# Turning rows 0 to 4 of a layer's input by VectorE blocks and a trip over DRAM instead of by TensorE

## The chip, the cores and the metric

One core of a Trainium2 chip runs the whole program. The metric is the device time of one execution in microseconds (us), as the median of several executions. Five engines work side by side: TensorE (PE, with its weight loads shown as PEld), VectorE (DVE), ScalarE (ACT), GpSimd (POOL) and SyncE (SP), which here only issues DMAs. The engines wait for one another by semaphores.

## The reference

A two-layer decoder trunk on 1024 prompt tokens and 32 sample tokens (8 sequences of 4), model width 1024, in float32. Layer 0 is a gated short convolution, layer 1 a gated linear recurrence with 8 heads of 128.

```python
h = rms_norm(x, norm_pre[i])
proj = h @ w_in                      # 1024 -> 4096
y = mixer(proj) @ w_out              # 1024 -> 1024
x = x + rms_norm(y, norm_post[i])
```

`rms_norm(x, g)` is `x * rsqrt(mean(x*x) + 1e-6) * g`. What the change touches lies between the layers: the first layer's `y = o @ w_out`, `x1 = x + rms_norm(y, norm_post[0])`, and then `h = rms_norm(x1, norm_pre[1])`, which is the second layer's input.

## The kernel before

**Layouts.** The products of layer 1 need h with the model's 1024 features on partitions (8 tiles k of 128 features) and tokens on the free axis. The first layer's output comes with tokens on partitions. So each row of 128 tokens (rows 0 to 7; 1024 tokens) has to be turned, 128 by 128 for each k, before layer 1 can read it. Every product is done in float32r with operands split into a high part (a rounding copy by ACT) and a low part (the difference, by DVE), three matmuls for one product.

**The stage around the change** (about 386 to 462 us of the span). TensorE works through rows 3 to 7 of `o @ w_out` (`products`, L837; 48 matmuls of 512 columns a row, for k = 0 to 7; rows 0 to 2 were done together with the arrival of the weights). Row i uses banks 2(i mod 3) and the next one, so it waits for event t1 of row i-3 (`V_PO`), after which DVE has read both banks. Between two values of k, `turn_rows(n)` (L854) is put in: 8 transposes of row n into banks 6 and 7. The order is written out by hand in `TURN`: turn 0 stands in row 3 behind k=3, turn 1 in row 4 behind k=3, turns 2 and 3 in rows 4 and 5 behind k=7, turn 4 in row 6 behind k=3, turn 5 in row 6 behind k=7, and turn 6 in row 7 behind k=7. Then come the value products of layer 1 (`FIRST`, L692, groups of 24 matmuls of 352 columns), and turn 7 stands behind the second of them. The fifth group is the first that reads the last tokens.

**DVE for each row i** (the loop that calls `scaled_y`): y times the post norm's weights in two halves (L2103, events t0 and t1), the inverse root (L2106), x1 = residual + scaled y (L2113), then `turned(i-1)` (L2128: the turned row i-1 read from PSUM, times the pre norm's weights, into `o_tr`), the second inverse root (L2159), the norm of the row into `o_n[i % 2]` (L2161, event xn), and `turned_lo(i-1)` (L2134, the low part). In row 6 two low parts of layer 1's weights are made too (`split_lo`, L1736), one ahead of the second root and one behind `turned_lo`.

**ACT for each row i**: the squares of y (L1413, two halves, from PSUM), the root (L1420), the squares of x1 (L1413), the second root (L1420, event sd2), `turned_hi(i-1)` (L1446), and then `squares_y(i+1)`. In row 6 the high parts of two weight tiles (L1207) stand ahead of the squares of x1. In row 7 the eviction of the first value group follows `turned_hi(6)`.

**SP, in order, for each row i**: wait for x1, store x1 to DRAM (L498), and for i up to 4 load the residual of row i+3 (L460) once row i is normed and its store is done. All its DMAs share one queue. `arena` is the SBUF tensor in which `o_x`, `o_n`, `o_t` and `o_tr` lie; `o_tr` has two buffers, as `o_n` has.

Of the kernel before, what the change touches and what calls it, by code (L numbers as in the profile page):

```python
# [95 lines left out]
def build(nc, x_prompt, x_sample, state_conv, state_hgrn, norm_pre, w_in, conv_w, lb_logits, onorm,  # L96
          w_out, norm_post, y_prompt, y_sample, conv_p, conv_s, hgrn_p, hgrn_s):
    ctx = ExitStack()
    with ctx:
# [3 lines left out]
        def sem(name):  # L103
            return ctx.enter_context(nc.semaphore(name))
# [210 lines left out]
        A_P2 = Events(sem("out2_act"), ["s0", "s1", "sd1"])  # L315
        V_P2 = Events(sem("out2_dve"), ["t0", "ms", "t1", "rs", "x"])
        first_half_x = sem("first_half_x")
        Q_PE = [Events(sem("sample_pe"), ["y", "n1", "n2", "tr"]), Events(sem("sample2_pe"), ["y", "n1"])]
        Q_ACT = [Events(sem("sample_act"), ["sq", "sd", "sq2", "sd2", "hi"]), Events(sem("sample2_act"), ["sq", "sd"])]
        Q_DVE = [Events(sem("sample_dve"), ["t", "rs", "x", "rs2", "xn", "g", "lo"]),  # L320
# [43 lines left out]
        def wsrc(w, col):  # L364
            return w[:, bass.ds(col, P)].rearrange("(k p) c -> p k c", p=P)
# [15 lines left out]

        def rows_of(i):
            return P if i < CK else NSAMP

        def quarter(q):
            return slice(q * QD, (q + 1) * QD), slice(q * NSAMP, (q + 1) * NSAMP)
# [13 lines left out]
        def _(sp):  # L400
            def load_w(n, src, slot, half, guard=True):

                if guard:
                    sp.wait_ge(w_lo, n - 1)
                sp.dma_start(wraw[:, slot], src).then_inc(w_in_s[slot], 16)
# [76 lines left out]
            sp.wait_ge(cout, 32)  # L482
            sp.dma_start(o_g, norm_post[0:1, :].broadcast_to([P, D])).then_inc(g_in, 16)

            QC, FC, VC, ZC = 0, D, 2 * D, 3 * D
            for i in range(CK):
                if i == 0:
                    for first in range(3):
                        load_x(first)
                    sp.wait_ge(Q_PE[0].sem, Q_PE[0].at(0, "y"))  # L490
                    load_w(NW2, wsrc(w_in[1], VC), 0, None)
                    load_w(NW2 + 1, wsrc(w_in[1], QC), 1, None)
                    sp.wait_ge(Q_DVE[0].sem, Q_DVE[0].at(0, "x"))
                    for q in range(4):
                        cols, own = quarter(q)
                        sp.dma_start(x1_dram[NP:T, cols], smp_x[0][own, :]).then_inc(smp_kept, 16)
                sp.wait_ge(V_PO.sem, V_PO.at(i, "x1"))
                sp.dma_start(x1_dram[i * P:i * P + rows_of(i), :], o_x[i % 3][0:rows_of(i), :]).then_inc(stored[i % 3], 16)  # L498
                if i + 3 < CK:
                    load_x(i + 3)  # L500
            load_w(NW2 + 2, wsrc(w_in[1], FC), 0, None)

            def move_values(h):
# [145 lines left out]
        def _(pe):  # L649
# [193 lines left out]
            def turn_rows(i):  # L843

                r = rows_of(i)
                pe.wait_ge(V_PO.sem, V_PO.at(i, "xn"))
                if i == 0:
                    pe.wait_ge(Q_DVE[0].sem, Q_DVE[0].at(0, "g"))
                if i:
                    pe.wait_ge(V_TR.sem, V_TR.at(i - 1, "gb"))  # L850
                for half, name in enumerate(("ta", "tb")):
                    for k in range(4):
                        kk = half * 4 + k
                        mm = nc.tensor.transpose(bank[6 + half][:, k * P:k * P + r],  # L854
                                                 o_n[i % 2][0:r, kk * P:(kk + 1) * P], ident[0:r, 0:r])
                    mm.then_inc(P_TR.now(name), 1)
# [35 lines left out]
            for cc in range(2):  # L892
                mm = nc.tensor.transpose(bank[7][:, (1 + cc) * P:(2 + cc) * P], smp_n[:, cc * P:(cc + 1) * P], ident[:, :])
            mm.then_inc(Q_PE[0].now("tr"), 1)
            TURN = {(3, 3): 0, (4, 3): 1, (4, 7): 2, (5, 7): 3, (6, 3): 4, (6, 7): 5, (7, 7): 6}
            for i in range(3, CK):
                pe.wait_ge(V_PO.sem, V_PO.at(i - 3, "t1"))
                for k in range(KT):
# [300 lines left out]
        def _(act):  # L1199
# [233 lines left out]
            def squares_y(i):  # L1433

                r = rows_of(i)
                if i >= 2:
                    act.wait_ge(P_TR.sem, P_TR.at(i - 2, "tb"))
                act.wait_ge(y_done, i + 1)
                for half in range(2):
                    square(bank[2 * (i % 3) + half][0:r, :], o_n[i % 2][:, half * HALF:(half + 1) * HALF], A_PO,  # L1440
                           f"s{half}", col(i, "ab"[half]), r)

            def turned_hi(i):
                r = rows_of(i)
# [284 lines left out]
        def _(dve):  # L1729
# [386 lines left out]
            def turned(i):  # L2116

                r = rows_of(i)
                dst = o_tr[i % 2].rearrange("p (k t) -> p k t", k=KT)
                if i >= 2:  # L2120
                    dve.wait_ge(A_TR.sem, A_TR.at(i - 2, "hi"))
                    dve.wait_ge(V_TR.sem, V_TR.at(i - 2, "lo"))
                for half, (name, g_name) in enumerate((("ta", "ga"), ("tb", "gb"))):
                    dve.wait_ge(P_TR.sem, P_TR.at(i, name))
                    src = bank[6 + half][:, :].rearrange("p (k t) -> p k t", k=4)[:, :, 0:r]
                    first = PRE + KT + 4 * half
                    g = cst[:, first:first + 4].unsqueeze(2).broadcast_to([P, 4, r])
                    V.tensor_tensor(dst[:, 4 * half:4 * half + 4, 0:r], src, g, ALU.mult).then_inc(V_TR.now(g_name), 1)  # L2128

            def turned_lo(i):  # L2130
                r = rows_of(i)
                hh, hl = planes(reg_a)
                dve.wait_ge(A_TR.sem, A_TR.at(i, "hi"))
                V.tensor_tensor(hl[:, :, i * P:i * P + r], o_tr[i % 2].rearrange("p (k t) -> p k t", k=KT)[:, :, 0:r],  # L2134
                                hh[:, :, i * P:i * P + r].bitcast(F32), ALU.subtract).then_inc(V_TR.now("lo"), 1)

# [6 lines left out]
            for i in range(CK):  # L2143
# [9 lines left out]
                    sample_next("xn")  # L2153
                elif i == 1:
                    sample_next("g")
                if i:
                    turned(i - 1)
                dve.wait_ge(A_PO.sem, A_PO.at(i, "sd2"))
                V.reciprocal(col(i, "rs2", r), col(i, "sd2", r)).then_inc(V_PO.now("rs2"), 1)  # L2159
                dve.wait_ge(V_PO.sem, V_PO.at(i, "rs2"))  # L2160
                V.tensor_scalar(o_n[i % 2][0:r, :], o_x[i % 3][0:r, :], col(i, "rs2", r), None,  # L2161
                                ALU.mult).then_inc(V_PO.now("xn"), 1)
                if i:
                    turned_lo(i - 1)
                if i == 1:
# [386 lines left out]
```

## Time and profile before

| | |
|---|---|
| median of 3 executions | 1027.96 us (1027.74 to 1028.17) |
| the profiled execution's own time | 1027.81 us |
| its span, first to last instruction | 1025.6 us |
| PE busy | 1018.9 us, 99% |
| DVE busy | 712.2 us, 69% |
| ACT busy | 419.1 us, 41% |
| granted TensorE clock | 0.999 |

The busy share of PE includes short overlaps at the end of pipelined matmuls, so it doesn't say that each matmul ran at its best rate; it says that hardly any time passed without one. The 2.2 us between span and time lie before the first and after the last instruction.

### The profile page before, as it was taken

Reading aid. Unit: us, or ns where it says so; the run is one execution under the profiler, and the core shown is the slowest. Engines: PE = TensorE matmul, PEld = TensorE weight load, DVE = VectorE, ACT = ScalarE, POOL = GpSimd, SP = SyncE. Lnnn points to the kernel's source line nnn. Section 1 sums busy time; section 2 is a strip of 40 time slices with the busy share of each in tenths; the row PEclk is TensorE's granted clock in tenths of the full one; section 3 lists DMA queues with packets and bytes.
Section 4 is the critical chain, followed back from the end, with each engine's and each line's share of the span. In section 5 each row is a group of like instructions: output and inputs, shape, how many; then the busy total and the mean of one; then the engine's idle time right before and its main releaser. Section 6 shows DMA issues by size and latency. Waiting matters only on the chain.

```text
span 1025.6 us, 20565 instructions
## 1 busy us (share of the span) xinstructions
PE 1018.9 (99%) x7915; PEld 970.4 (95%) x7915; DVE 712.2 (69%) x1282; ACT 419.1 (41%) x844; POOL 18.3 (2%) x45
## 2 busy tenths in 40 slices
PE   9999999999999999999999999999999999999998
PEld 8999999999999978889999999999999999997886
DVE  7899677677776925762758769495867859596355
ACT  7444333333433614443334444434534344383222
POOL 1000000000000000000000000000000000000000
PEclk9999999999999999999999999999999999999999
DMA  8003121112111344322213122231322122153064
GB/s 255 22 22 82 42 80 43 41 42 80 41 41 47 118 145 141 117 82 59 63 53 85 50 54 64 66 79 41 84 61 52 53 71 75 61 173 108 29 240 170
DMA packets 130368, 82.96 MB, mean 81 GB/s; under 512 B 37781, under 2 KB 121702, under 8 KB 130326
## 3 DMA queue, kind: packets, MB, share of 16 engines
q1 hardware_dynamic: 112438, 73.39, 24.0%
q10 hardware_dynamic: 17888, 8.98, 3.1%
q8 instruction: 29, 0.48, 0.2%
q14 instruction: 13, 0.11, 0.0%
HBM read 64.72 MB, written 13.44 MB: 76 GB/s over the span
## 4 chain that ended last, share of the span: by engine, by line
PE 95%; DVE 3%; ACT 1%; issue 1%; POOL 0%; ACTq 0%; POOLq 0%; DVEq 0%
PE bank L692 35%; PE bank L749 28%; PE bank L837 14%; PE bank L717 4%; PE bank L1092 3%; PE bank L931 2%; PE bank L1041 1%; PE bank L1048 1%; PE bank L1050 1%; PE bank L819 1%; PE bank L1035 1%; PE bank L854 1%; PE bank L953 1%; PE bank L926 1%; PE bank L945 1%; DVE o_raw L1800 1%
## 5 line engine op out<-in xcount | busy, mean ns | idle before, releaser
L692 PE MATMUL bank<-reg_a,wsplit 128*128 128x352 f32 x2304 | 380.4, 324 | 0.0
L692 PEld LDWEIGHTS bank<-reg_a,wsplit 128*128 128x128 f32 x2304 | 368.6, 188 | 1.4
L749 PE MATMUL bank<-reg_a,wsplit 128*128 128x264 f32 x1344 | 165.6, 284 | 0.0
L749 PEld LDWEIGHTS bank<-reg_a,wsplit 128*128 128x128 f32 x1344 | 164.1, 188 | 0.1
L749 PE MATMUL bank<-reg_b,w_ring 128*128 128x264 f32 x1008 | 124.6, 284 | 0.0
L749 PEld LDWEIGHTS bank<-reg_b,w_ring 128*128 128x128 f32 x1008 | 123.3, 188 | 0.0
L837 PE MATMUL bank<-reg_b,reg_a 128*128 128x512 f32 x288 | 69.3, 396 | 0.0
L837 PEld LDWEIGHTS bank<-reg_b,reg_a 128*128 128x128 f32 x288 | 53.7, 188 | 12.7 <-issue 0.4
L1951 DVE TENSOR_TENSOR arena<-arena,bank 128x264 f32<-128x264 f32 x84 | 34.8, 427 | 34.2 <-PE bank L749 33.0
L1313 ACT ACTIVATE arena<-bank 128x264 f32<-128x264 f32 x84 | 32.2, 390 | 54.6 <-PE bank L749 49.9
L1291 ACT ACTIVATE w_ring<-wraw 128x512 fp32r<-128x512 f32 x42 | 26.1, 631 | 69.0 <-PE bank L749 69.0
L2439 DVE COPY arena<-bank 128x128 f32<-128x128 f32 x8 | 2.3, 292 | 66.6 <-PE bank L1041 66.6
L1291 ACT ACTIVATE wsplit<-wraw 128x512 fp32r<-128x512 f32 x42 | 25.0, 627 | 49.6 <-DMA wraw<-in_w_in 36.6
L1736 DVE TENSOR_TENSOR wsplit<-wraw,wsplit 128x1024 fp32r<-128x1024 f32 x32 | 39.0, 1218 | 4.7 <-ACT wsplit L1207 4.7
L837 PE MATMUL bank<-reg_a,reg_b 128*128 128x512 f32 x168 | 39.9, 395 | 0.0
L837 PEld LDWEIGHTS bank<-reg_a,reg_b 128*128 128x128 f32 x168 | 31.6, 188 | 7.5
L1207 ACT ACTIVATE wsplit<-wraw 128x1024 fp32r<-128x1024 f32 x32 | 33.7, 1054 | 0.7 <-PE bank L837 0.7
L2103 DVE TENSOR_TENSOR arena<-bank,arena 128x512 f32<-128x512 f32 x24 | 16.3, 686 | 25.1 <-ACT arena L1413 25.1
L1465 ACT ACTIVATE arena<-bank 128x352 f32<-128x352 f32 x24 | 11.1, 464 | 55.1 <-PE bank L692 55.0
L2188 DVE TENSOR_TENSOR arena<-arena,r_tt 128x512 f32<-128x512 f32 x32 | 22.2, 693 | 16.3 <-PE bank L926 8.6
L1899 DVE TENSOR_TENSOR w_ring<-wraw,w_ring 128x512 fp32r<-128x512 f32 x42 | 28.8, 690 | 6.5 <-ACT w_ring L1291 6.5
L2449 DVE TENSOR_REDUCE small<-arena 128x4 f32<-128x512 f32 x16 | 10.2, 681 | 31.4 <-ACT arena L1626 31.4
(297 smaller groups left out, 1494.6 us busy)
## 6 DMA issues: line engine op xcount, KB each, us to landing
wraw<-in_w_in SPq DMA_DIRECT2D x64, 512.0 KB, 4.1
first_x<-in_x_prompt SPq DMA_DIRECT2D x8, 512.0 KB, 7.0
wraw<-in_w_out SPq DMA_DIRECT2D x8, 512.0 KB, 4.0
w_out_raw<-in_w_out SPq DMA_DIRECT2D x8, 512.0 KB, 5.5
arena<-in_w_out SPq DMA_DIRECT2D x8, 512.0 KB, 6.4
arena<-in_x_prompt SPq DMA_DIRECT2D x8, 512.0 KB, 3.3
x_scratch<-arena SPq DMA_DIRECT2D x8, 512.0 KB, 2.6
arena<-arena SPq DMA_DIRECT2D x128, 32.0 KB, 1.9
```

The costliest lines, as they stand in the source:

```text
L692: mm = nc.tensor.matmul(bank[b][:, 0:CH], w[wi][:, k, :], rhs[hi], start=(k == 0 and i == 0), stop=(k == KT - 1 and i == 2))
L717: mm = nc.tensor.matmul(bank[b][:, 0:QT], w[wi][:, k, :], src[hi][:, k % KH, cols], start=(k == 0 and i == 0), stop=(k == KT - 1 and i == 2))
L749: mm = nc.tensor.matmul(bank[banks[q]][:, 0:QT], w[wi][:, k, :], B_OP[name][hi][:, k, q * QT:(q + 1) * QT], start=(start and k == 0 and i ...
L837: mm = nc.tensor.matmul(bank[b][0:r, :], src[side][:, k, i * P:i * P + r], w[wi][:, half * HALF:(half + 1) * HALF], start=(start and side ...
L1092: mm = nc.tensor.matmul(bank[PART_BANK[n]][:, :], o1[side][:, k, i * P:(i + 1) * P], wout_tile(reg_a, k)[wi][:, half * HALF:(half + 1) * H ...
L1207: A(wsplit[:, s, 0] if dst is None else dst, wraw[:, s], ACT.Copy).then_inc(w_hi, 1)
L1291: A(w_block(name)[0], A_RAW[name], ACT.Copy).then_inc(W_HI.now(name), 1)
L1313: A(dst[:, q * QT:(q + 1) * QT], bank[banks[q]][:, 0:QT], ACT.Copy).then_inc(C_ACT.now(f"{what}{s}{q}"), 1)
L1736: V.tensor_tensor(d, wraw[:, s], h.bitcast(F32), ALU.subtract).then_inc(w_lo, 1)
L1899: V.tensor_tensor(lo, A_RAW[name], hi.bitcast(F32), ALU.subtract).then_inc(W_LO.now(name), 1)
L1951: V.tensor_tensor(dst[:, cols], src[:, cols], bank[banks[q]][:, 0:QT], ALU.add).then_inc(C_DVE.now(f"{what}{s}{q}"), 1)
L2188: V.tensor_tensor(pairs(to[0][:, 0:NP], m)[1], pairs(queries[:, 0:NP], m)[1], tl.unsqueeze(2).broadcast_to([P, nb, m]), ALU.mult)
```

## The change

For rows 0 to 4 (`BLOCK_ROWS = 5`) the turn is no longer done by TensorE. DVE writes the norm of the row with its columns permuted (by quarter d, tile k, column c of 32) and then turns it in 32 by 32 blocks in place. SP stores the result to a DRAM scratch (512 KB, one of two) and loads it back in four DMAs of 128 KB, each to 32 partitions with runs of 1 KB, which puts the blocks where they belong; `o_tr` then holds the turned row as (block b, tile k, token t). `turned(i)` for these rows is one multiply by the pre norm's weights in place. For rows i up to 5, `turned(i-1)` stays ahead of the second inverse root of row i; for rows 6 and 7 it moves behind that root. Rows 5, 6 and 7 are still turned by TensorE: turn 5 stands now in row 7 behind k=3 (before: row 6 behind k=7), turns 6 and 7 stay where they were. In the diff, `keep_blocks` and `load_turned` are SP's, the waits on `blocks_kept` ahead of the squares are ACT's, and what follows them is DVE's.

```diff
+BLOCK_ROWS = 5
+        row_blocks = [nc.dram_tensor(f"row_blocks{i}", (P, D), F32, kind="Internal").ap() for i in range(2)]
+        def in_blocks(ap):
+            return ap.rearrange("p k (b t) -> p k b t", b=NQD)
+        def turned_in(i):
+            return o_tr[i % 2].rearrange("p (b k t) -> p k b t", b=NQD, k=KT)
...
+            def keep_blocks(i):
+                sp.wait_ge(row_turned, i + 1)
+                if i >= 2:
+                    sp.wait_ge(row_landed[i % 2], 64 * (i // 2))
+                sp.dma_start(row_blocks[i % 2], o_n[i % 2]).then_inc(blocks_kept[i % 2], 16)
+            def load_turned(i):
+                sp.wait_ge(blocks_kept[i % 2], 16 * (i // 2 + 1))
+                if i == 1:
+                    sp.wait_ge(Q_DVE[0].sem, Q_DVE[0].at(0, "lo"))
+                elif i >= 2:
+                    sp.wait_ge(V_TR.sem, V_TR.at(i - 2, "lo"))
+                src = row_blocks[i % 2].rearrange("(b c) (d n) -> d c b n", b=NQD, d=NQD)
+                for d in range(NQD):
+                    dst = o_tr[i % 2][d * BLK:(d + 1) * BLK, :].rearrange("c (b n) -> c b n", b=NQD)
+                    sp.dma_start(dst, src[d]).then_inc(row_landed[i % 2], 16)
...
                 sp.dma_start(x1_dram[i * P:i * P + rows_of(i), :], o_x[i % 3][0:rows_of(i), :]).then_inc(stored[i % 3], 16)
+                if i < BLOCK_ROWS:
+                    keep_blocks(i)
                 if i + 3 < CK:
                     load_x(i + 3)
+                if i < BLOCK_ROWS:
+                    load_turned(i)
...
-            TURN = {(3, 3): 0, (4, 3): 1, (4, 7): 2, (5, 7): 3, (6, 3): 4, (6, 7): 5, (7, 7): 6}
+            TURN = {(7, 3): 5, (7, 7): 6}
...
                 if i >= 2:
-                    act.wait_ge(P_TR.sem, P_TR.at(i - 2, "tb"))
+                    if i - 2 < BLOCK_ROWS:
+                        act.wait_ge(blocks_kept[i % 2], 16 * (i // 2))
+                    else:
+                        act.wait_ge(P_TR.sem, P_TR.at(i - 2 - BLOCK_ROWS, "tb"))
...
+                if i < BLOCK_ROWS:
+                    dve.wait_ge(row_landed[i % 2], 64 * (i // 2 + 1))
+                    own = o_tr[i % 2].rearrange("p (b k t) -> p b k t", b=NQD, k=KT)
+                    g = cst[:, PRE + KT:PRE + 2 * KT].unsqueeze(1).unsqueeze(3).broadcast_to([P, NQD, KT, BLK])
+                    V.tensor_tensor(own, own, g, ALU.mult).then_inc(*V_TR.many("ga", "gb"))
+                    return
...
-                if i:
+                if 0 < i <= BLOCK_ROWS:
                     turned(i - 1)
                 dve.wait_ge(A_PO.sem, A_PO.at(i, "sd2"))
                 V.reciprocal(col(i, "rs2", r), col(i, "sd2", r)).then_inc(V_PO.now("rs2"), 1)
                 dve.wait_ge(V_PO.sem, V_PO.at(i, "rs2"))
-                V.tensor_scalar(o_n[i % 2][0:r, :], o_x[i % 3][0:r, :], col(i, "rs2", r), None,
-                                ALU.mult).then_inc(V_PO.now("xn"), 1)
+                if i > BLOCK_ROWS:
+                    turned(i - 1)
+                if i < BLOCK_ROWS:
+                    by_quarter = o_n[i % 2].rearrange("p (d k c) -> p k d c", d=NQD, k=KT)
+                    V.tensor_scalar(by_quarter, o_x[i % 3].rearrange("p (k d c) -> p k d c", d=NQD, k=KT), col(i, "rs2", r), None,
+                                    ALU.mult).then_inc(V_PO.now("xn"), 1)
+                    dve.wait_ge(V_PO.sem, V_PO.at(i, "xn"))
+                    V.transpose(o_n[i % 2], o_n[i % 2]).then_inc(row_turned, 1)
+                else:
+                    V.tensor_scalar(o_n[i % 2][0:r, :], o_x[i % 3][0:r, :], col(i, "rs2", r), None,
+                                    ALU.mult).then_inc(V_PO.now("xn"), 1)
```

The high and low parts of rows 0 to 4 (`turned_hi`, `turned_lo`) are the same single instructions, now reading `o_tr` in its block order and writing tokens in order.

## Rows read from the trace of the kernel before

**Rows 1.** The page, part 4: the chain that ended last, by engine.
```profile
PE 95%; DVE 3%; ACT 1%; issue 1%; POOL 0%; ACTq 0%; POOLq 0%; DVEq 0%
```

**Rows 2.** Busy time by stretch: stretch, length, busy us, granted clock, DMA share, GB/s.
```profile
386.00:461.50 75.50, 75.50 (x378) 63.50 (x376) 49.26 (x85) 33.20 (x77) 0.00 (x0) 1.00 0.32 109
461.50:1025.60 564.10, 559.44 (x4477) 531.81 (x4475) 381.02 (x697) 230.33 (x489) 13.22 (x16) 1.00 0.28 82
```

**Rows 3.** Timeline of PE, rows 5 to 7: start, us, what, count [idle before <-releaser].
```profile
427.19 1.04 PE L854 MATMUL bank<-ident,arena 128*128 128x128 f32 x8
427.98 3.04 PE L837 MATMUL bank<-wsplit,reg_a 128*128 128x512 f32 x12
...
433.65 1.04 PE L854 MATMUL bank<-ident,arena 128*128 128x128 f32 x8
...
440.89 3.04 PE L837 MATMUL bank<-wsplit,reg_a 128*128 128x512 f32 x12
...
452.14 1.03 PE L854 MATMUL bank<-ident,arena 128*128 128x128 f32 x8
...
460.71 1.03 PE L854 MATMUL bank<-ident,arena 128*128 128x128 f32 x8
```

**Rows 4.** Timeline of DVE: the norm of row 0, then rows 1, 6 and 7.
```profile
390.60 0.75 DVE L2161 TENSOR_SCALAR arena<-arena,small 128x1024 f32<-128x1024 f32 x1
...
397.29 1.29 DVE L2128 TENSOR_TENSOR arena<-bank,cst 128x512 f32<-128x512 f32 x2 [2.94 <-PE bank L854]
398.50 0.15 DVE L2159 RECIPROCAL small<-small 128x1 f32<-128x1 f32 x1
398.68 0.76 DVE L2161 TENSOR_SCALAR arena<-arena,small 128x1024 f32<-128x1024 f32 x1
399.71 1.23 DVE L2134 TENSOR_TENSOR reg_a<-arena,reg_a 128x1024 fp32r<-128x1024 f32 x1 [0.27 <-ACT reg_a L1446]
...
441.15 0.69 DVE L2103 TENSOR_TENSOR arena<-bank,arena 128x512 f32<-128x512 f32 x1 [3.12 <-ACT arena L1413]
...
442.61 1.29 DVE L2113 SCALAR_TENSOR_TENSOR arena<-arena,small 128x1024 f32<-128x1024 f32 x1
...
453.19 0.69 DVE L2103 TENSOR_TENSOR arena<-bank,arena 128x512 f32<-128x512 f32 x1 [3.45 <-ACT arena L1413]
...
457.69 0.76 DVE L2161 TENSOR_SCALAR arena<-arena,small 128x1024 f32<-128x1024 f32 x1
```

**Rows 5.** Timeline of ACT in row 6.
```profile
441.94 0.29 ACT L1420 ACTIVATE small<-small,eps 128x1 f32<-128x1 f32 x1 [0.32 <-DVE small L2101]
442.57 1.06 ACT L1207 ACTIVATE wsplit<-wraw 128x1024 fp32r<-128x1024 f32 x1 [0.34 <-PE bank L837]
...
444.94 1.04 ACT L1413 ACTIVATE arena<-arena 128x1024 f32<-128x1024 f32 x1
...
446.10 0.30 ACT L1420 ACTIVATE small<-small,eps 128x1 f32<-128x1 f32 x1
```

**Rows 6.** Page, part 6: DMA issues, count, KB each, median us from issue to landing.
```profile
arena<-in_x_prompt SPq DMA_DIRECT2D x8, 512.0 KB, 3.3
x_scratch<-arena SPq DMA_DIRECT2D x8, 512.0 KB, 2.6
arena<-arena SPq DMA_DIRECT2D x128, 32.0 KB, 1.9
```

**Rows 7.** The same part of all DMA issues: the residual of the sample rows.
```profile
arena<-in_x_sample SPq DMA_DIRECT2D x4, 32.0 KB, 3.3
```

**Rows 8.** Timeline of SP: start, and time that the issuing takes.
```profile
361.45 0.43 SPq L476 DMA_DIRECT2D arena<-in_x_sample  x1
361.92 0.42 SPq L477 DMA_DIRECT2D arena<-in_norm_post  x1
...
481.00 11.58 SPq L510 DMA_DIRECT2D arena<-arena  x16
```

**Rows 9.** Groups of instructions by line: the in-place block transpose of 1024 columns.
```profile
L2331 DVE STREAM_TRANSPOSE arena<-arena 128x1024 f32<-128x1024 f32 x8 | 9.9, 1236 | 0.0
```

More of the change, by code:

```diff
@@ L317, in build @@
         first_half_x = sem("first_half_x")
+        row_turned = sem("rows_turned_in_blocks")
+        blocks_kept, row_landed = [[sem(f"{n}{i}") for i in range(2)] for n in ("row_blocks_kept", "turned_row_in")]
         Q_PE = [Events(sem("sample_pe"), ["y", "n1", "n2", "tr"]), Events(sem("sample2_pe"), ["y", "n1"])]
@@ L846, in turn_rows @@
                 pe.wait_ge(V_PO.sem, V_PO.at(i, "xn"))
-                if i == 0:
+                if i == BLOCK_ROWS:
                     pe.wait_ge(Q_DVE[0].sem, Q_DVE[0].at(0, "g"))
-                if i:
+                else:
                     pe.wait_ge(V_TR.sem, V_TR.at(i - 1, "gb"))
@@ L1445, in turned_hi @@
                 act.wait_ge(V_TR.sem, V_TR.at(i, "gb"))
+                if i < BLOCK_ROWS:
+                    A(in_blocks(planes(reg_a)[0][:, :, i * P:i * P + r]), turned_in(i), ACT.Copy).then_inc(A_TR.now("hi"), 1)
+                    return
                 A(planes(reg_a)[0][:, :, i * P:i * P + r], o_tr[i % 2].rearrange("p (k t) -> p k t", k=KT)[:, :, 0:r],
@@ L2119, in turned @@
                 dst = o_tr[i % 2].rearrange("p (k t) -> p k t", k=KT)
-                if i >= 2:
-                    dve.wait_ge(A_TR.sem, A_TR.at(i - 2, "hi"))
-                    dve.wait_ge(V_TR.sem, V_TR.at(i - 2, "lo"))
+                if i < BLOCK_ROWS:
[3 more added lines that the diff above has]
+                    V.tensor_tensor(own, own, g, ALU.mult).then_inc(*V_TR.many("ga", "gb"))
+                    return
+                dve.wait_ge(A_TR.sem, A_TR.at(i - 2, "hi"))
+                dve.wait_ge(V_TR.sem, V_TR.at(i - 2, "lo"))
                 for half, (name, g_name) in enumerate((("ta", "ga"), ("tb", "gb"))):
-                    dve.wait_ge(P_TR.sem, P_TR.at(i, name))
+                    dve.wait_ge(P_TR.sem, P_TR.at(i - BLOCK_ROWS, name))
                     src = bank[6 + half][:, :].rearrange("p (k t) -> p k t", k=4)[:, :, 0:r]
@@ L2133, in turned_lo @@
                 dve.wait_ge(A_TR.sem, A_TR.at(i, "hi"))
+                if i < BLOCK_ROWS:
+                    at = slice(i * P, (i + 1) * P)
+                    V.tensor_tensor(in_blocks(hl[:, :, at]), turned_in(i), in_blocks(hh[:, :, at].bitcast(F32)),
+                                    ALU.subtract).then_inc(V_TR.now("lo"), 1)
+                    return
                 V.tensor_tensor(hl[:, :, i * P:i * P + r], o_tr[i % 2].rearrange("p (k t) -> p k t", k=KT)[:, :, 0:r],
@@ L2155, in _ @@
                     sample_next("g")
-                if i:
+                if 0 < i <= BLOCK_ROWS:
                     turned(i - 1)
@@ L2160, in _ @@
                 dve.wait_ge(V_PO.sem, V_PO.at(i, "rs2"))
-                V.tensor_scalar(o_n[i % 2][0:r, :], o_x[i % 3][0:r, :], col(i, "rs2", r), None,
-                                ALU.mult).then_inc(V_PO.now("xn"), 1)
+                if i > BLOCK_ROWS:
+                    turned(i - 1)
+                if i < BLOCK_ROWS:
+                    by_quarter = o_n[i % 2].rearrange("p (d k c) -> p k d c", d=NQD, k=KT)
[3 more added lines that the diff above has]
+                    V.transpose(o_n[i % 2], o_n[i % 2]).then_inc(row_turned, 1)
+                else:
+                    V.tensor_scalar(o_n[i % 2][0:r, :], o_x[i % 3][0:r, :], col(i, "rs2", r), None,
+                                    ALU.mult).then_inc(V_PO.now("xn"), 1)
                 if i:
```

## The prediction

> **What bounds the kernel now.** Read the chain of waits first: 95% of it is PE [rows 1]. So a saved microsecond of PE time counts in full, if PE isn't made to wait instead, and anything off PE counts only where PE comes to wait for it. Busy time by stretch shows that the stage of the change has no hole in it: PE is busy for 75.50 of 75.50 us at a granted clock of 1.00, with DVE at 49.26 us and ACT at 33.20 [rows 2]. The reader is to see two things there. The turns stand inside a full PE, so each costs its own time; and DVE has a third of the stage idle, which in the timelines is waiting for PE: 2.94 us ahead of the weighting of turned row 0, 3.12 and 3.45 us ahead of the first half of rows 6 and 7 [rows 4]. Behind the stage PE is busy for 559.44 of 564.10 us [rows 2], so what the stage gains or loses reaches the end nearly whole; I pass it on at 1.
>
> **What PE saves.** A turn costs the distance from its start to the start of the next products, 427.98 - 427.19 = 0.79 us [rows 3]; its 1.04 us of busy time overlaps by the rest. Five of eight turns go: 5 x 0.79 = 3.95 us. That is the floor of the gain, 1027.81 - 3.95 = 1023.9 by the profiled execution's time. Nothing else on PE changes.
>
> PE's own schedule without waits follows. Row 7 began at 440.89 with turns 0 to 5 behind it; now it has none of them behind it, so it begins at 440.89 - 6 x 0.79 = 436.15. From a row's start to behind k=3 it is 433.65 - 427.98 = 5.67 us, so turn 5 comes up at 441.8. Turn 6 comes up 0.79 + (452.14 - 440.89 - 5.67) = 6.4 us after turn 5 starts, and turn 7 as before 460.71 - 452.14 = 8.57 us after turn 6 starts [rows 3]. Turn 7 is where I measure: it was at 460.71, and unhindered would be at 456.76.
>
> **What each row now costs on the way through DVE, SP and DRAM.** A turn by TensorE needed only the norm and came back when PE got to it. Now row i's turned data must be weighted ahead of row i+1's second root, so everything on DVE behind that multiply, row i+1's norm too, waits for the trip. That makes a chain over five rows. Call T(i) the end of the block transpose of row i, and R the time from T(i) to the landing of its fourth load.
>
> T(0): the norm of row 0 ends at 390.60 + 0.75 = 391.35 [rows 4]; a block transpose of 1024 columns takes 1.24 [rows 9]; with 0.04 for the handoff, T(0) = 392.63. From landing to T(i+1) there are one multiply over 1024 columns, 1.23 as for the low part, less an overlap of 0.08 with what follows (1.29 - 1.21 between 397.29 and 398.50), the reciprocal to norm distance of 0.18, the norm of 0.75 with 0.04, and the transpose of 1.24 [rows 4, 9]: 1.15 + 0.18 + 0.79 + 1.24 = 3.36. The old multiplies, two of 512 columns, took 1.29 together [rows 4]; DVE's work for a row grows by the transpose alone, 5 x 1.24 us, beside PE.
>
> R: SP's wake-up 0.05; the store of 512 KB to DRAM, 2.6 from issue to landing, as eight such stores show [rows 6]; two waits, 0.1; four issues of which the last starts three distances after the first. The distance is 0.47 for DMAs of 32 rows with runs of 1 KB from DRAM, and 11.58/16 = 0.72 for the sixteen between partitions of SBUF with short runs [rows 8]. Mine are of the first kind: 1.41. The last load of 128 KB lands in something between 1.9 (32 KB within SBUF) and 3.3 us (512 KB from DRAM, or 32 KB from DRAM among other loads) [rows 6, 7]. In a line between 1.9 and 3.3 by size it would be 2.2; with shorter runs I take 2.3. With 0.05 to DVE, R = 0.05 + 2.6 + 0.1 + 1.41 + 2.3 + 0.05 = 6.5. With the best ends it is 2.6 + 0.1 + 1.41 + 1.9 + 0.1 = 6.1; with 3.3 for the landing 7.5; with 0.72 for the distance too, 8.3. The residual load that SP issues between the store and the loads is in the same queue; it was issued anyway and is through before the first load moves bytes, so I price it at 0, 0.3 in R at worst.
>
> Beside the trip DVE does the low part of row i-1 and x1 of row i+1: 1.2 and 441.15 to 442.61 + 1.29, that is 2.75 us, together 4.0 [rows 4]. That is under R, so it hides; and rows 3 to 5 of the products are done well before DVE asks for them. The waits of PE for t1 of the row three back keep more than 6 us of slack: t1 of row 4 comes at about T(3) + 2.6 = 424.8, and row 7 asks at 436.15.
>
> So xn(5), the norm of row 5, ends at X = T(0) + 4(R + 3.36) + R + 1.15 + 0.18 + 0.75 = 408.15 + 5R. With R = 6.5, X = 440.65, 1.1 us before turn 5 comes up. No wait there.
>
> **The last three rows.** After X, DVE waits for ACT's high part of row 4, as it did 1.13 us from 397.29 + 1.29 to 399.71 [rows 4]: the low part ends at X + 1.5, and the first half of row 6 starts at X + 1.42. Call that A. ACT's root ends at A + 1.08; the two weight copies (1.06 each) no longer wait for PE, so they end at A + 3.1; squares and second root take 446.40 - 444.94 = 1.46 more, A + 4.56 [rows 5]. Then the reciprocal, and behind it the two halves of turned row 5, 1.21, which used to stand in the shade of ACT, and the norm: xn(6) ends at A + 4.56 + 0.04 + 0.18 + 1.21 + 0.75 = A + 6.7, that is X + 8.1. PE wants turn 6 at 441.8 + 6.4 = 448.2 and gets it at 440.65 + 8.1 = 448.8: 0.6 us of stall. Then the high part of row 5 on ACT and the low part on DVE end 2.3 after A + 5.95, a weight's low part (1.2) follows, and row 7 starts at A + 9.4. Row 7 takes 457.69 + 0.76 - 453.19 = 5.26 as before plus 1.21 for the turned row 6 that now stands behind its second root [rows 4]: xn(7) ends at A + 9.4 + 6.45 = X + 17.3. So turn 7 starts at X + 17.3 = 457.95, against 460.71: -2.76 us. Two of DVE's moved weightings and the shared chain eat 1.2 of the 3.95 us.
>
> In general the change is worth 408.15 + 5R + 17.3 - 460.71 = 5R - 35.25 us, and not less than -3.95. Each 0.1 us of R is 0.5 us. It breaks even at R = 7.05; the floor is reached at R = 6.26. The time of the profiled execution would be 1027.81 - 2.76 = 1025.05. The median of the runs shown is 0.15 higher, so 1025.2.
>
> **Where the skill speaks.** A store to DRAM took 2.6 us from issue to landing in this trace [rows 6]. The Trainium skill (DMA: Bandwidth & Descriptors, section on the anatomy of one DMA) fits 2.0 us plus the bytes over 436 GB/s for a DMA from the other, software path, most of the fixed part being the write's receipt. By its figure, as an estimate, the store would be 3.2 and R 7.1, and the change worth +0.3; the trace has eight stores at 2.6, so this carries only a part of the chance of the slow trip.
>
> The norm's write is now permuted, runs of 32 columns. The trace shows 0.75 us for the contiguous one, and 1.29 for an instruction of the same 1024 columns at what looks like half the rate (x1 of row 6) [rows 4]; a permuted one has no row. I take 0.75 as the nearest row; 1.29 is the other end and would cost 5 x 0.54 = 2.7 us, because the norm stands in the chain in rows 0 to 4. The Trainium skill (VectorE: DVE Perf Modes, section on the mode that uses both read ports) asks of such an instruction only one source in SBUF and an even outermost dimension; by it the write keeps 0.75, and no row here shows it.
>
> **Rivals.**
> - The floor. If the last load lands within 2.0 us, R is 6.26 or less, no turn waits, and the time is 1024.0. For it: such small transfers within SBUF land in 1.9. Against: those from DRAM took 3.3, though among others [rows 6, 7].
> - A trip as long as what it replaces. With R near 7 (the queue's other transfers push the loads by 0.3 to 0.5), or R = 6.5 and a norm at half rate (-2.76 + 2.7), the gain is given back by the stall at turn 7: 1027 to 1029.
> - The trip over DRAM becomes the bound: slower. Place: PE's wait for the norm of row 5 at turn 5, and then for those of rows 6 and 7. From R = 7.05 the change costs 5 times what is above. At R = 7.5, the landing of a 512 KB load, turn 5 would wait till X = 445.65, 3.9 us, and the whole is +2.25: 1030.2. With the issue distance of 0.72, +6: 1034. For it: all five trips stand in the sum for X, with nothing beside them that could take up a delay, and X is only 1.1 us ahead of turn 5. Against: the stores' 2.6 is firm, and four loads share the traffic of one.
> - That TensorE's time doesn't shrink by 0.79 a turn is hardly open: the transposes are simply gone.
>
> **How the numbers follow.** The forecast (R from 6.3 to 6.85, -3.75 to -1.0) gets 0.46, the floor 0.14, the give-back (R to 7.2 or the slow norm, -1.0 to +1.0) 0.19, the slow trip 0.21, of which 0.05 is for the skill's fixed cost. What a measurement can tell from no change is put at 0.2%, 2.06 us. Faster by more needs R under 6.64: the floor and 0.36 of the forecast, 0.50. Within it: 0.10 of the forecast, the give-back, and 0.04 of the slow trip, 0.33. Slower: 0.17. The range goes from the floor, 1023.9, to the R of 7.5, 1030.2; beyond the upper end I leave 0.14 or so, below the lower hardly anything. The forecast's own range is 1024.2 to 1027.0.
>
> **What would show it.** PE: three groups of 8 transposes of rows, not eight, and 3.95 us less of products' delay up to row 7, which starts at about 436.2. DVE: five block transposes of 1.24 in this stage, and five idle times ahead of the weighting of about R - 4 = 2.5 us, ended by a DMA. SP: the store of the blocks landing in 2.6, four issues 0.47 apart, the last landing in 2.3. PE idle: nothing at turn 5, about 0.6 us at turn 6, 0.6 us more at turn 7, released by DVE. It is wrong if the norm of row 5 ends behind 442, if the norm in rows 0 to 4 takes more than 0.8 us, or if a wait shows in rows 3 to 7 of the products themselves.

## The result and the profile after

The changed kernel takes 1031.43 us (median of 8 executions, 1030.77 to 1031.88) against 1027.96 before: ratio 1.0033, 95% interval 1.0022 to 1.0044. It is slower by 3.5 us; forecast were 2.8 us faster, and the time lies 1.2 us above the range. The profiled execution took 1031.67, 3.86 more than that of before.

PE (TensorE) bounds the kernel, so read it first. Timeline of PE in the changed kernel, from row 7 on (L887 are the turns, L870 the products; in brackets the idle time ahead and what ended it):
```profile
435.93 2.96 PE L870 MATMUL bank<-wsplit,reg_a 128*128 128x512 f32 x12
...
447.23 1.97 PE L887 MATMUL bank<-ident,arena 128*128 128x128 f32 x8 [5.54 <-DVE arena L2219]
448.85 7.57 PE L870 MATMUL bank<-reg_b,reg_a 128*128 128x512 f32 x24
456.26 1.03 PE L887 MATMUL bank<-ident,arena 128*128 128x128 f32 x8
...
464.82 1.03 PE L887 MATMUL bank<-ident,arena 128*128 128x128 f32 x8
```
The saving is there: row 7 starts at 435.93, where 436.15 was worked out from [rows 3]. Then TensorE stands idle for 5.54 us ahead of turn 5, waiting for the norm of row 5 (L2219). Turn 5 takes 1.62 us and the products behind it 7.41, where 0.79 and 5.58 are normal [rows 3]. Turn 7 starts at 464.82, before at 460.71: 4.1 us later. Of these, 0.15 are an offset that the stage already starts with (the norm of row 0 begins at 390.75 instead of 390.60).

Busy time by stretch, columns as in [rows 2], shows why those two are slow:
```profile
441.60:447.20 5.60, 0.09 (x1) 0.00 (x0) 2.18 (x4) 2.29 (x4) 0.00 (x0) 0.88 0.64 210
447.20:448.85 1.65, 1.62 (x8) 1.62 (x9) 1.41 (x2) 1.36 (x5) 0.00 (x0) 0.50 0.00 0
448.85:452.00 3.15, 3.15 (x10) 2.47 (x9) 3.12 (x6) 2.63 (x4) 0.00 (x0) 0.50 0.00 0
452.00:456.30 4.30, 4.30 (x19) 3.46 (x18) 3.30 (x6) 1.95 (x4) 0.00 (x0) 0.92 0.30 122
```
The granted clock falls to 0.50 (1.2 of 2.4 GHz) while TensorE is idle, and stays there when it works again. The mean of 0.92 over the last stretch puts the return to full speed at about 452.7 (4.30 x 0.08 / 0.50 = 0.7), 5.5 us after the wait ended.

The chain of waits of the changed kernel (start, us, what) goes over DRAM in this stage. `row_blocks<-arena` is the store of a row's blocks, `arena<-row_blocks` the last of its four loads. Pieces of rows 0, 1, 3 and 4:
```profile
392.81 3.42 DMA row_blocks<-arena
...
396.62 1.82 SPq L512
...
398.96 2.67 DMA arena<-row_blocks
401.72 1.22 DVE arena L2163
403.05 0.77 DVE arena L2214
403.84 1.26 DVE arena L2217
405.11 2.86 DMA row_blocks<-arena
407.99 0.32 SPq L512
...
409.30 3.03 DMA arena<-row_blocks
412.42 1.22 DVE arena L2163
...
426.26 3.30 DMA row_blocks<-arena
...
430.89 3.62 DMA arena<-row_blocks
434.60 1.23 DVE arena L2163
...
438.00 2.87 DMA row_blocks<-arena
...
442.19 2.81 DMA arena<-row_blocks
445.09 1.23 DVE arena L2163
446.42 0.77 DVE arena L2219
```
That is the chain that was foreseen (store, issues, last load, weighting L2163, norm L2214, block transpose L2217), with longer pieces. The trip R, from the end of the transpose (0.02 ahead of the store) to the weighting, was 8.93, 7.33, 7.07, 8.37 and 7.11 us for rows 0 to 4, together 38.8 where 5 x 6.5 = 32.5 was forecast. DVE's idle time ahead of the weightings is in the summary of waits (us in total, times, longest), where five times 2.5 was forecast:
```profile
DVE arena L2163 <- DMA arena<-row_blocks: 20.5, 5, 6.0
```
And the DMA issues of the stage (390 to 470 us), count, size, median landing, answer to [rows 6]:
```profile
row_blocks<-arena SPq DMA_DIRECT2D x5, 512.0 KB, 2.9
...
arena<-row_blocks SPq DMA_DIRECT2D x20, 128.0 KB, 2.8
```

### The profile page after: what moved, and what is told of

Read it like the earlier page. It is cut to its first block, busy times and chain, and to the rows that moved or that the text cites. A ratio compares the mean times of both kernels' runs of the same rounds, so it can differ in the third digit from the quotient of the medians.

```text
span 1029.8 us, 20516 instructions
## 1 busy us (share of the span) xinstructions
PE 1017.3 (99%) x7875; PEld 968.0 (94%) x7875; DVE 716.7 (70%) x1282; ACT 418.6 (41%) x844; POOL 18.2 (2%) x45
## 4 chain that ended last, share of the span: by engine, by line
PE 89%; DVE 5%; DMA 3%; ACT 1%; issue 1%; SPq 1%; ACTq 0%; DVEq 0%
PE bank L725 34%; PE bank L782 28%; PE bank L870 8%; PE bank L750 4%; PE bank L1125 3%; PE bank L964 2%; DMA row_blocks<-arena 1%; DMA arena<-row_blocks 1%; PE bank L1074 1%; PE bank L1081 1%; PE bank L1083 1%; SPq L512 1%; PE bank L852 1%; PE bank L1068 1%; PE bank L986 1%
## 5 line engine op out<-in xcount | busy, mean ns | idle before, releaser
L870 PE MATMUL bank<-reg_b,reg_a 128*128 128x512 f32 x288 | 70.6, 403 | 0.0
L870 PEld LDWEIGHTS bank<-reg_b,reg_a 128*128 128x128 f32 x288 | 55.2, 193 | 13.3 <-issue 0.4
L870 PE MATMUL bank<-reg_a,reg_b 128*128 128x512 f32 x168 | 39.9, 395 | 0.0
L870 PEld LDWEIGHTS bank<-reg_a,reg_b 128*128 128x128 f32 x168 | 31.6, 188 | 7.5
L1504 ACT ACTIVATE arena<-bank 128x352 f32<-128x352 f32 x24 | 11.1, 464 | 55.1 <-PE bank L725 55.0
L1496 ACT ACTIVATE arena<-bank 128x352 f32<-128x352 f32 x24 | 11.1, 464 | 49.4 <-PE bank L725 49.4
```

The lines of the kernel that those rows point to most:

```text
L870: mm = nc.tensor.matmul(bank[b][0:r, :], src[side][:, k, i * P:i * P + r], w[wi][:, half * HALF:(half + 1) * HALF], start=(start and side ...
```

## The experiments

Theory A: each row's norm waits for the trip of the row before it, five times; that makes the norm of row 5 late, and it and DVE's work behind it set turns 5 to 7. Rivals: the low clock is the cost by itself; DVE's extra work is; SP or the queue is. The kernels differ from the changed kernel only in what is shown or said below. In e8 and e12 theory A has a second part, that the trip is long because it shares the DMA queue and engines. Ratios are to the kernel before, each with its 95% interval.

| kernel | what it changes | us | ratio |
|---|---|---|---|
| changed kernel | | 1031.43 | 1.0033 (1.0022 to 1.0044) |
| e1_fill | transposes of the identity in TensorE's wait at turn 5 | 1031.28 | 1.0031 (1.0019 to 1.0043) |
| e2_notrip | no store of the blocks, no loads | 1023.79 | 0.9960 (0.9946 to 0.9974) |
| e3_order | weighting behind the next row's block transpose | 1025.18 | 0.9973 (0.9962 to 0.9983) |
| e4_rows3 | three rows by blocks | 1028.32 | 1.0005 (0.9996 to 1.0014) |
| e5_order_ahead | e3, and weightings of rows 5 and 6 ahead of the root | 1023.66 | 0.9957 (0.9944 to 0.9971) |
| e6_ahead | weightings of rows 5 and 6 ahead of the root | 1031.03 | 1.0029 (1.0019 to 1.0038) |
| e7_ahead_fill | e6 and e1 | 1029.88 | 1.0019 (1.0010 to 1.0028) |
| e8_residual_last | the residual's load behind the four loads | 1030.48 | 1.0020 (1.0010 to 1.0031) |
| e9_two_queues | two of the four loads on ScalarE's queue | 1031.31 | 1.0030 (1.0019 to 1.0042) |
| e10_rows6 | e5 with six rows by blocks | 1027.48 | 0.9997 (0.9988 to 1.0006) |
| e11_rows3_ahead | e4 with all weightings ahead of the root | 1025.39 | 0.9978 (0.9968 to 0.9988) |
| e12_trip_alone | the DMAs beside the trips made small | 1028.47 | 1.0011 (1.0002 to 1.0020) |

**e2_notrip: is the trip all of it?**
```diff
-                    keep_blocks(i)
...
-                    load_turned(i)
...
-                    dve.wait_ge(row_landed[i % 2], 64 * (i // 2 + 1))
+                    dve.wait_ge(row_turned, i + 1)
...
-                    V.tensor_tensor(own, own, g, ALU.mult).then_inc(*V_TR.many("ga", "gb"))
+                    from_n = o_n[i % 2].rearrange("p (b k t) -> p b k t", b=NQD, k=KT)
+                    V.tensor_tensor(own, from_n, g, ALU.mult).then_inc(*V_TR.many("ga", "gb"))
```
The lines not shown are waits: they keep `o_tr` until its last readers are done, and ACT's squares wait for the weighting, as there is no store to wait for.

> Left out: the store of the blocks and the four loads of rows 0 to 4; the weighting reads the row's own blocks, so the values of the second layer's input are misplaced. DVE, ACT and TensorE do the same instructions. Theory A, the trip is all that is wrong: the full saving of five turns, 1027.96 - 3.95 = 1024.0, no wait of TensorE in rows 3 to 7. Rival, DVE's longer work (five block transposes, moved weightings) is part of the loss: 1025 to 1027, with a wait at turns 6 and 7.

1023.79. All five turns' 3.95 us come out, and no wait stands at turns 5 to 7; turn 7 starts at
```profile
457.01 1.03 PE L887 MATMUL bank<-ident,arena 128*128 128x128 f32 x8
```
The block transposes and the moved weightings cost nothing while the norms come early.

**e3_order: the place of the weighting.**
```diff
-                if 0 < i <= BLOCK_ROWS:
+                if i == BLOCK_ROWS:
                     turned(i - 1)
...
                     V.transpose(o_n[i % 2], o_n[i % 2]).then_inc(row_turned, 1)
+                    if i:
+                        turned(i - 1)
```


> The weighting of row i-1 stands behind the block transpose of row i for i = 1 to 4 (for row 5 it stays ahead of the root), so a row's trip runs beside the next row's norm. Theory A, the loss is that each row's norm waits for the trip of the row before: the period falls from R + 3.36 = 11.1 to DVE's own 9.9 us, norm of row 5 at 441.3 instead of 447.2, no stall at turn 5, 1.3 us at turn 6, turn 7 at 458.6: 1025.5. Rival, the trip is as late as before because SP or the DMA queue is the chain's bound: 1030 to 1031.4.

1025.18, where 1025.5 was expected. Timeline of DVE for row 2, and of PE for turns 5 to 7:
```profile
410.81 1.25 DVE L2217 STREAM_TRANSPOSE arena<-arena 128x1024 f32<-128x1024 f32 x1
411.98 1.18 DVE L2163 TENSOR_TENSOR arena<-arena,cst 128x1024 f32<-128x1024 f32 x1
```
```profile
441.87 1.04 PE L887 MATMUL bank<-ident,arena 128*128 128x128 f32 x8
449.63 1.09 PE L887 MATMUL bank<-ident,arena 128*128 128x128 f32 x8 [1.12 <-DVE arena L2221]
458.80 1.09 PE L887 MATMUL bank<-ident,arena 128*128 128x128 f32 x8 [0.39 <-DVE arena L2221]
```
The weighting at 411.98 follows the transpose with no idle time: the data of row 1 have landed while row 2 was normed. From row 2 on the transposes are 9.9 us apart (410.81, 420.70, 430.59) instead of 10.4 to 12.3. Waits for a landing are left only for rows 0 and 4 (2.17 and 1.61 us). The trips aren't shorter: the store lands in 2.9 us and a load in 2.9 in the median, as against 2.9 and 2.8 in the changed kernel. So the loss is their place in front of the norm, and the waits left at turns 6 and 7 (1.12, 0.39) are DVE's own chain behind row 5, expected as 1.3 at turn 6 and turn 7 at 458.6.

**e5_order_ahead: those two as well.** e3_order with `if i >= BLOCK_ROWS: turned(i - 1)` ahead of the second root, and nothing between root and norm.

> e3_order, and the weighting of turned rows 5 and 6 ahead of the second root of rows 6 and 7, as in the kernel before. Theory A: the weightings (1.2 us each) go back into DVE's wait for ACT, so the norm of row 6 is ready 1.2 and that of row 7 2.4 us earlier than in e3_order (449.6 and 458.8, where TensorE waited 1.1 and 0.4 us); nothing waits any more and the whole saving of five turns shows: 1027.94 - 3.95 = 1024.0. Rival, TensorE's waits at turns 6 and 7 come from elsewhere (the low parts, ACT's order): 1025.2 as e3_order.

1023.66, 4.3 us under the kernel before, and the lowest of all:
```profile
441.46 1.03 PE L887 MATMUL bank<-ident,arena 128*128 128x128 f32 x8
448.15 1.09 PE L887 MATMUL bank<-ident,arena 128*128 128x128 f32 x8
456.77 1.03 PE L887 MATMUL bank<-ident,arena 128*128 128x128 f32 x8
```
Turn 7 is at 456.77, where a TensorE without waits was put at 456.76. Two differences of 0.3 cancel in that: row 7 began at 435.86, for 436.15, and turn 6 still waited some 0.3 us for the norm of row 6, which ended at 448.10 (447.34 + 0.76). So "nothing waits any more" holds to 0.3 us.

**e1_fill, e6_ahead, e7_ahead_fill: the clock.** e1_fill puts transposes of the identity ahead of the wait; e6_ahead moves the weighting of rows 5 and 6 ahead of the root; e7_ahead_fill does both.
```diff
-                pe.wait_ge(V_PO.sem, V_PO.at(i, "xn"))
                 if i == BLOCK_ROWS:
                     pe.wait_ge(Q_DVE[0].sem, Q_DVE[0].at(0, "g"))
-                else:
+                    for _ in range(50):
+                        nc.tensor.transpose(bank[6][:, 0:P], ident[:, :], ident[:, :])
+                pe.wait_ge(V_PO.sem, V_PO.at(i, "xn"))
+                if i > BLOCK_ROWS:
                     pe.wait_ge(V_TR.sem, V_TR.at(i - 1, "gb"))
```


> 50 transposes of the identity stand on TensorE ahead of its wait for the norm of row 5 (5.0 of the 5.54 us it idled). Theory A, DVE's chain behind the norm of row 5 sets the end and the clock drop behind the idle time is mostly covered by it: turn 7 can't start before the norm of row 7 (464.3 in the changed kernel, where it started at 464.8), so 1031.1, 0.4 to 0.5 less than the changed kernel's 1031.4, with turn 5 at 0.79 us, the clock at 1.00 throughout, and new waits at turns 6 and 7. Rival B, the clock drop is the cost by itself: turn 5 and the products behind it took 1.62 + 7.41 us at clock 0.5 instead of 0.79 + 5.58, so 2.6 less, 1028.8.

1031.28, where theory A had 1031.1 and the rival 1028.8. Timeline of PE (with the added lines, turns are L889):
```profile
441.49 5.62 PE L882 MATMUL bank<-ident 128*128 128x128 f32 x50
447.27 1.09 PE L889 MATMUL bank<-ident,arena 128*128 128x128 f32 x8 [0.16 <-DVE arena L2221]
...
455.21 1.09 PE L889 MATMUL bank<-ident,arena 128*128 128x128 f32 x8 [1.25 <-DVE arena L2221]
...
464.38 1.09 PE L889 MATMUL bank<-ident,arena 128*128 128x128 f32 x8 [0.39 <-DVE arena L2221]
```
At full clock nearly all of the 2.6 us come back: 1.8 as waits (0.16, 1.25, 0.39) and the rest in the matmuls around them (turn 5 takes 0.85 instead of 0.79, the products behind it 5.84 instead of 5.58). Turn 7 moves from 464.82 to 464.38 only. From the norm of row 5 (447.2) to turn 7 it is 17.2 us, and in e3_order 458.80 - 441.64 = 17.2 too; 17.3 was worked out.

> The changed kernel with only the weighting of turned rows 5 and 6 moved back ahead of the root. Theory A: turn 5 still waits for the norm of row 5 (447.2); behind it TensorE is at half clock, and its own pace (turn 6 at 456.3, turn 7 at 464.8) is behind DVE's, so an earlier norm gives nothing: 1031.4 as the changed kernel. Rival, DVE's chain alone sets turns 6 and 7: up to 2.4 less, 1029.0.

> e6_ahead with the 50 transposes of the identity ahead of turn 5. Now neither DVE nor a low clock should hold turns 6 and 7: turn 6 at 447.3 + 6.4 = 453.7 and turn 7 at 462.3, 2.5 us ahead of the changed kernel: 1029.0, and the difference to e6_ahead (2.4) is the price of the low clock behind the idle time by itself. Rival, the clock isn't what made turn 5 and the products behind it slow: 1031.

1031.03, for 1031.4, and 1029.88, for 1029.0. With less of DVE's chain in the way the clock has a price, 1.15 us between the medians. That is too little, because the fill of e7 ran over: its norm of row 5 ended at 446.54 (in e6 at 446.59), but turn 5 started at 447.03, when the 50 transposes were through. From the start of turn 5 to that of turn 7 it is 17.4 (446.65 to 464.05) in e6, at a granted clock of 0.50 from 446.6 to 448.3, against 15.5 (447.03 to 462.56) at 1.00 in e7: 1.9 us for the low clock. I had put it at 2.4; turn 6 of e7 still waited 0.31 for DVE.

**e4_rows3 and e11_rows3_ahead: fewer rows.** `BLOCK_ROWS = 3`, turn 3 at (5, 7), turns 4 to 7 as before the change. e11 has all weightings ahead of the root.

> Three rows (0 to 2) by blocks instead of five; turn 3 behind row 5's products (as before the change), turns 4 to 7 where the kernel before had them. Theory A: the norm of row 3 is ready at 425.0, turn 3 comes up at 424.8, all later ones have over 2 us; three turns saved, 3 x 0.79 = 2.37 us: 1025.6. Rival, the trip also costs something beside the waits of TensorE for norms (shared DMA queue, later x1 stores, clock): 1026.5 or more.

1028.32: theory A's 1025.6 was missed by 2.7 us, and two waits of TensorE that it didn't have make up 2.3 of them:
```profile
432.36 1.09 PE L887 MATMUL bank<-ident,arena 128*128 128x128 f32 x8 [0.91 <-DVE arena L2219]
...
440.40 1.09 PE L887 MATMUL bank<-ident,arena 128*128 128x128 f32 x8 [1.35 <-DVE arena L2219]
```
I had counted "over 2 us" of slack from the kernel before, where the weighting stood in DVE's wait for ACT; behind the root it is on the path of every norm.

> e4_rows3 (three rows by blocks) with the weighting of turned rows ahead of the second root for rows 4 to 7 too, as in the kernel before. Theory A: what ate e4_rows3's saving was TensorE's waits of 0.9 and 1.35 us at turns 4 and 5, where DVE needed 8.0 us a row with the weighting behind the root; ahead of it 6.8, less than the 7.2 that TensorE takes between them: three turns saved, 1025.6. Rival, the waits come from the trip of row 2 or the low parts: 1027.5 to 1028.3.

1025.39, for 1025.6 (one of the ten executions took 2027.68, which is not explained; the ratio leaves it out). So the second half of the change, the weighting of turned rows behind the root, costs 2.9 us here, more than the 2.4 that three turns save. Its price depends on what stands beside it: 1.5 between e3 and e5, and only 0.4 between the changed kernel and e6.

**e8_residual_last, e9_two_queues, e12_trip_alone: what makes the trip long.** e8 swaps `load_x(i + 3)` and `load_turned(i)`; e9 gives two loads to ScalarE's queue; e12 shrinks the other DMAs.
```diff
+                    act.wait_ge(blocks_kept[n % 2], 16 * (n // 2 + 1))
...
+                    for d in range(2, NQD):
+                        dst = o_tr[n % 2][d * BLK:(d + 1) * BLK, :].rearrange("c (b n) -> c b n", b=NQD)
+                        act.dma_start(dst, blocks[d]).then_inc(row_landed[n % 2], 16)
...
+                n = 16 if i >= 3 else D
...
+                n = 16 if 1 <= i <= 5 else D
```
The first two pieces are e9's, on ScalarE; the last two are e12's, the columns of the residual's load and of the store of x1.

> The changed kernel with the residual's load of 512 KB issued behind the four loads of the turned row instead of between the store of the blocks and them. If part of the trip is contention with it (store landing in 2.9 instead of 2.6, last load in 2.8 to 3.0 instead of 2.3), R falls from 7.8 by 0.25 to 0.8 us, five times that at the norm of row 5, and the time is 1027.4 to 1030.2. Rival, the landings are what they are (a load of short runs from DRAM takes 2.8 with nothing beside it): 1031.4.

1030.48, just outside the 1027.4 to 1030.2 of theory A, with executions from 1028.44 to 1033.72. The profiled one is the slowest of the eight. In its chain the store of row 1 is shorter, but not that of row 3, and the last load of row 4 is long:
```profile
404.24 2.61 DMA row_blocks<-arena
...
425.03 4.37 DMA row_blocks<-arena
...
442.03 4.86 DMA arena<-row_blocks
```
The residual between store and loads costs the store 0.25 us (2.86 to 2.61). In this execution that is lost again in rows with one long landing, 4.37 and 4.86. What the faster executions did is not known: none of them has a trace.

> The changed kernel, with two of the four loads of each turned row issued by ScalarE on its own DMA queue (in its gap between the first root and the squares of x1 of the next row), beside SP's two. Theory A, every 0.1 us of a row's trip is 0.5 at the norm of row 5: the last issue comes 0.94 us earlier, R falls from 7.8 to 6.8, the norm of row 5 from 447.2 to 442.5, turn 7 from 464.8 to 459.8: 1026.4. Rival, issue isn't what sets the landing (the DMA engines are): R falls by 0.3 or less, 1030 to 1031.

1031.31, against 1026.4 by theory A and 1030 to 1031 by the rival: the rival held. With both pairs issued at once the last issue starts 0.9 us earlier, but the last load then takes 0.7 (row 1) and 1.4 us (row 2) longer to land than in the changed kernel. The chain's pieces for these rows:
```profile
407.15 0.36 ACTq L1532
...
407.53 3.74 DMA arena<-row_blocks
...
417.65 0.36 ACTq L1532
...
418.03 4.17 DMA arena<-row_blocks
```

> The changed kernel with nearly nothing beside the trips in the DMA queue: the residual loads of rows 3 to 7 and the x1 stores of rows 1 to 5 move 16 of 1024 columns (left out: the other columns, so the values of those rows are wrong; the scratch of x1 is filled once, early, from the input). Theory A, the trip is longer than 6.5 us because it shares the DMA engines: the store lands in 2.6, the last load in 2.3, R is 6.4 but for the rows with an instruction load in them, 6.8 in the mean instead of 7.8, and the time 1026.4. Rival, four loads of short runs from DRAM land in 2.8 by themselves: R 7.3, 1029.

1028.47, between the two (1026.4 and 1029), nearer the rival. From its chain, row 2 and the last load of row 4:
```profile
415.13 2.65 DMA row_blocks<-arena
...
419.12 2.78 DMA arena<-row_blocks
...
440.33 2.74 DMA arena<-row_blocks
```
With hardly anything beside it the store takes 2.64 or 2.65 in four rows (3.27 in row 3), but the last load still 2.52, 3.18, 2.78, 2.83 and 2.74. R was 7.8, 7.3, 6.9, 7.6 and 6.8. In a normal row (1, 2, 4) that is 7.0, as against 7.2 in the changed kernel and 6.5 assumed: 0.2 is company, all of it at the store, and 0.5 stays without company, a last load of 2.9 in the mean where 2.3 was assumed, less 0.1 of issues. No kernel varied the run length or the number of partitions, so what makes such a load take 2.9 isn't shown. The median mixes two kinds of execution: four of the eleven kept a granted clock of 1.0 (1027.62 to 1028.73), seven had 0.996 to 0.998 (1028.36 to 1031.33).

**e10_rows6: how far it goes.** e5_order_ahead with `BLOCK_ROWS = 6` and `TURN = {(7, 7): 6}`.

> e5_order_ahead with six rows by blocks, only turns 6 and 7 on TensorE. Theory A: the saving per row is 0.79, but the norm of row 6 now hangs on DVE's 9.9 us a row and on the trip of row 5, ready at about 451.3, where TensorE asks for it at 447.1: a wait of 4.2 us, turn 7 at 459.9 or, if the clock falls behind that wait as it did behind 5.5 us, at 462.5: 1026.8 to 1029.5, against e5_order_ahead's 1023.7. Rival, there is still slack and a sixth turn is saved: 1022.9.

1027.48, inside the expected 1026.8 to 1029.5, with executions from 1025.69 to 1029.4. The profiled one, the fastest, waited 3.05 us at turn 6 (expected: 4.2) and kept its clock. One other had its granted clock of 0.999 (1025.74); the remaining nine had 0.996 to 0.998 and took 1026.86 to 1029.4. A sixth row by blocks costs more than it saves: e5 takes 1023.66.

## Why the prediction was wrong

- **What bounds the kernel, what PE saves, how the stage's loss reaches the end:** right. Row 7 at 435.93 for 436.15; e2 and e5 reach 1023.79 and 1023.66 for a floor of 1023.9.
- **The chain through the trips:** right as a mechanism. The formula for the norm of row 5, 408.15 plus the sum of R, gives 447.0 with the measured trips; it was at 446.42 + 0.75 = 447.17, of which 0.15 is the stage's offset. The prediction had named a norm of row 5 behind 442 as a sign that it is wrong. The 3.36 of DVE is there too (401.72 to 405.09 is 3.37).
- **R: the step that failed, by its size, taken five times.** The sum R = 6.5 was too small by 1.26 in the mean. In a normal row (1, 2, 4) R is 7.2: the store 2.86 (2.6 assumed; the residual's load, priced at 0, costs 0.25 by e8), the issues 1.31 to the last one's start (1.41 assumed), the last load 2.77 to 3.03 (2.3 assumed). Rows 0 and 3 have 8.93 and 8.37. I had taken 1.9 for 32 KB within SBUF as one end of a line through 3.3 for 512 KB [rows 6], while the row nearest in kind, 32 KB from DRAM, already said 3.3 [rows 7]. That makes 6.3 us in all five, against 1.1 us of room.
- **The store wasn't "firm", and the trace of the kernel before said so.** The prediction read the median of [rows 6] as "eight stores at 2.6". The summary of that line (L498) gives min, median and max, and SP's timeline shows what stood beside the last:
```profile
DMA to landing us min/median/max: 2.6/2.6/3.4
...
456.33 1.53 SPq L405 DMA_DIRECT2D wraw<-in_w_in  x2
```
  The eighth store, issued at 455.97, took 3.4. It is the only one behind which other DMAs (two loads of 512 KB, the first at 456.33) were issued while it was under way, and that is how the residual's load stands behind each store of blocks. Nor was the residual through before the loads: in row 1 of the changed kernel it was issued at 405.56 and took 3.9, so it landed 1.5 us behind the issue of the first load (407.99).
- **The slow trip as a rival** was the mechanism that came true, at an R of 7.76, with 0.21 of the chance. By 5R - 35.25 it is +3.6; the medians differ by 3.5. That this fits to 0.1 us is partly luck: turn 7 moved by 4.1 (3.6, 0.15 of offset and 0.4 of the clock), the profiled executions differ by 3.86. The range ended at R = 7.5 for every row, and neither it nor any row of mine foresaw that two of five trips would be longer by over a microsecond.
- **The last three rows:** 17.3 us from the norm of row 5 to turn 7; 17.2 in e1 and e3. The 1.2 us that the weightings behind the root would cost show as 1.12 + 0.39 in e3 and are down to 0.3 in e5. In the changed kernel these waits didn't show, because a slow TensorE filled them: 464.82 is 17.6 behind the norm.
- **Not foreseen: the clock.** I let TensorE idle 3.9 us in the rival without asking what it does afterwards. It costs 0.4 us at turn 7 here (0.15 between the medians), since DVE's chain covers the rest (e1), and would have cost up to 1.9 with less of that cover (e6, e7).
- **The skill's two places.** The Trainium skill (DMA: Bandwidth & Descriptors, the anatomy of one DMA) would have made the store 3.2 us, as an estimate by its fit for the software path; it took 2.65 nearly alone (e12) and 2.86 in a normal row of the changed kernel, so the measurement decides against it. Only rows 0 and 3, at 3.42 and 3.30, were longer, so the R of 7.1 estimated from it was nearer the measured 7.8 for other reasons. The Trainium skill (VectorE: DVE Perf Modes, the mode with both read ports) had the permuted norm at full rate; it took 0.75 (L2214), and so the trace agrees.

What stays open: why rows 0 and 3 are longer. In the changed kernel, e5, e8 and e12 they hold a 16 KB instruction load, at about 396 to 397 and 426 to 428 us. In row 0 issuing one load took 1.82 us and not 0.43, and long landings lie there; but e8's 4.86 in row 4 has none beside it. Coincidence is shown, cause not; no kernel moved those instruction loads. In e12, with little beside them, the two rows were still 0.8 and 0.6 us over the normal ones.

## What to carry to other kernels

When a step is moved from a full engine to a route over DMA, ask what stands behind the first instruction that waits for its return: put another row's work there before it, and the route's length no longer counts (e3, e5: the same trips, 6 to 8 us less). Where a latency is taken n times in a chain, n times its error is the error of the answer; take it from the row nearest in kind, not by a line through two sizes, and hold it against the room that there is. A filler step that hides in a wait (here the weighting ahead of a root) is free only there. And where the profile's page gives a median, look at the slowest of the group and at what stood beside it.

## What the runs showed of the hardware

- After 3.1 us of idle TensorE in e12 and 5.5 in the changed kernel the granted clock was 0.50 for the next stretch; after 3.05 us in e10's profiled execution it stayed 1.00. It fell at different times within the idle stretch: by the mean of 0.86 over 442.00 to 445.30 at about 444.4 in e12, 2.2 us into it; by the mean of 0.88 over 441.60 to 447.20 at about 445.9 in the changed kernel, 4.2 us into it. First e12, then e10:
```profile
442.00:445.30 3.30, 0.22 (x1) 0.00 (x0) 2.05 (x3) 0.87 (x1) 0.00 (x0) 0.86 0.07 10
445.30:446.90 1.60, 1.59 (x8) 1.59 (x9) 1.38 (x2) 1.34 (x5) 0.00 (x0) 0.50 0.00 0
...
447.10:450.20 3.10, 0.05 (x2) 0.01 (x1) 3.00 (x4) 2.36 (x5) 0.00 (x0) 1.00 0.42 169
450.20:455.00 4.80, 4.80 (x33) 4.80 (x34) 4.57 (x7) 1.61 (x6) 0.00 (x0) 1.00 0.00 0
```
- Four loads issued two by two on two queues landed hardly earlier, or later, than four in a row on one: from the start of the first issue to the last landing it was 4.1 and 4.6 us for rows 1 and 2 of e9, and 4.3 (407.99 to 409.30 + 3.03) and 4.1 (418.69 to 420.00 + 2.77) for those of the changed kernel.
- A 512 KB store to DRAM with nothing issued behind it landed in 2.6 or 2.7 us seven times out of seven in the kernel before; the eighth, with two 512 KB loads behind it, the first by 0.36 us, took 3.4. In the changed kernel, with one such load 0.43 us behind it, it was 2.86 (row 2).
- DVE multiplied 1024 columns in a permuted order (blocks of 32 columns) at the rate of contiguous ones: 0.75 us for one source (L2214), 1.22 for two (L2163).
